# The scores of dense head group A as two split fp32r products over 128 partitions instead of one fp32 product over 64

## The chip, the cores and the metric

The kernel runs on one core of a Trainium2 chip. Its engines are named as in the profile: PE is TensorE (matrix products), with PEld its weight loads, DVE is VectorE, ACT is ScalarE, POOL is GpSimd, SP is SyncE, which issues the DMAs. The metric is the device time of one execution in microseconds; lower is better. Three runs of the kernel before took 1313.1, 1313.77 and 1316.71 us, median 1313.77.

## The reference

Two layers over 512 tokens of width 1024, all float32. Layer 0 mixes with attention, layer 1 with a recurrent block; each is followed by a SwiGLU feed-forward block, and a final RMS norm ends it. Only the attention's group A matters here: 8 query heads and 2 key heads of 64, each normalised per head, rotated by position, dense softmax over all 512 keys.

```python
a_q = _axial_rope(_rmsnorm(a_q, q_norm), row, col)
a_k = _axial_rope(_rmsnorm(a_k, k_norm), row, col)
...
s = jnp.einsum('bqgrd,bkgd->bgrqk', q_blk, k).astype(jnp.float32)
p = jax.nn.softmax(s, axis=-1).astype(v.dtype)
return jnp.einsum('bgrqk,bkgd->bqgrd', p, v)
```

Group B computes three dilated sliding-window attentions of 8 heads each from the same input projection and merges them by their softmax denominators.

## The kernel before

Every large product with weights is a split product, `mm3`: both operands are cut into a high part rounded to fp32r and a low part, the rest, and PE adds three fp32r products (high x high, high x low, low x high). A weight chunk comes by DMA into one of four stage buffers; ACT copies it to `w_hi` (L548), POOL subtracts to get `w_lo` (L488), PE waits for `chunk_lo` and uses it, and `chunk_used` lets ACT overwrite the slot. ACT and POOL convert chunk c + 4 while PE is at chunk c.

The order of work is written out by hand, one program per engine, in steps that are the weight chunks. The input projection is done in four head pairs p = 0 to 3 of 24 chunks (steps j = 0 to 23), and the attention is laid between the chunks. `A_SCORES = {10: 0, 13: 1, 16: 2, 19: 3}` puts the four score steps of group A (block c of 128 queries, two heads each) at steps 10, 13, 16 and 19 of pair p, `A_TURN` the transposes of their probabilities three steps later. `B_SCORES` puts the band scores of pair p - 1 at steps 0, 2, 4 and 6. Four more pieces of group B and of the output projection follow as p = 4. So there are 16 score steps of group A. A score step is, on PE, two fp32 products (one for each head of the pair: 64 partitions of `aq_f`, 128 queries, times 64 partitions of `ak`, 512 keys) into two banks; on DVE the maximum over both banks (`a_step`); on ACT two exponentials (`a_exps`); on DVE the normalisation (`a_normalise`); on PE the transposes (`a_turn`). The transposes of step c - 1 stand right ahead of the scores of step c on PE.

`aq_f` holds the rotated queries of pair p, two heads over 128 partitions. `ak` holds the two key heads, each copied by ACT (L675, two copies at step 9 and two at step 11 of pair 0) onto both halves of the partitions, so that either head of a pair finds its keys on its own partitions. DVE rotates the queries of the next pair at step 15 (`aq_rope`).

POOL and DVE also rotate group B's queries and keys of the pair: products with sine and cosine on POOL (L497, L503), a shuffle (L1098) and a sum on DVE (`rope_add`: `bq` L1109, `bkf` L1116, `bkn` L1111). The last `bkn` sum stands at step 22, and the band scores at step 0 of the next pair (L1600) wait for it (`roped`).

Of the kernel before, what the change touches and what calls it, by code (L numbers as in the profile page):

```python
# [5 lines left out]
P = 128  # L6
D = 1024
T = 512
KD = D // P
NC = T // P  # L10
# [199 lines left out]
def build(nc, A, out):  # L210
# [4 lines left out]
    with ctx:  # L215
# [4 lines left out]
        def at(name, off, shape, dt=f32):  # L220
            return nc.alloc_sbuf_tensor_at(name, [P] + list(shape), dt, offset=base + int(off))
# [45 lines left out]
        vf, bvf = at("vf", Z + 70.5 * K, [5 * P]), at("bvf", Z + 73 * K, [5, P])  # L267
        bvn = at("bvn", Z + 75.5 * K, [NC, 2, P])
        aq_f = at("aq_f", Z + 79.5 * K, [4, T])
        ak, av = at("ak", Z + 87.5 * K, [2, T]), at("av", Z + 91.5 * K, [NC, P])  # L270
        o_hi, o_lo = at("o_hi", Z + 93.5 * K, [KD, T], f32r), at("o_lo", Z + 109.5 * K, [KD, T], f32r)
        table = at("table", Z + 125.5 * K, [K_ALL - K_COSA])

# [26 lines left out]
        def sem(name):  # L300
            return ctx.enter_context(nc.semaphore(name))
# [13 lines left out]
        spilled, x_back = sem("spilled"), sem("x_back")  # L315
        half_ones_set, v_f_in, k_f_in, sq_done, aq_scaled, v_a_turned, av_in = (sem(n) for n in (
            "half_ones_set", "v_f_in", "k_f_in", "sq_done", "aq_scaled", "v_a_turned", "av_in"))
        ssq_ready, qk_ms, qk_sqrt, k_diag, k_rb, k_roped, ak_done, aq_roped = (sem(n) for n in (
            "ssq_ready", "qk_ms", "qk_sqrt", "k_diag", "k_rb", "k_roped", "ak_done", "aq_roped"))
        qk_in, sin_done, cos_done, roped, v_in = (sem(n) for n in ("qk_in", "sin_done", "cos_done", "roped", "v_in"))  # L320
        a_scored, a_bias, a_exp, a_prob = (sem(n) for n in ("a_scored", "a_bias", "a_exp", "a_prob"))
        b_scored, b_masked, b_bias, b_exp, b_prob = (sem(n) for n in ("b_scored", "b_masked", "b_bias", "b_exp", "b_prob"))
# [39 lines left out]
        def turned_near(hh, b):  # L362

            near = ptn[:, hh, :, :].rearrange("p g (c b i) -> p g c b i", c=NC, b=4)
            return near[:, :, :, b, :], ps[:, 2 + hh, 256:512].rearrange("p (g c i) -> p g c i", g=2, c=NC)

        block = ctx.enter_context(nc.Block())


# [166 lines left out]
        def _(act):  # L536
# [112 lines left out]
            def first_pair(j):  # L649

                if j == 0:
                    act.wait_ge(chunk_used, C_PAIR)
                    act.wait_ge(params_ready, 1)
                    act.activation(v_f[:, :], ps[:, 5, :], ACT.Copy).then_inc(v_f_in, 1)
                    act.activation(k_f[:, :], ps[:, 4, :], ACT.Copy, scale=qk_gain[:, 1:2]).then_inc(k_f_in, 1)
                    act.activation(sq_qk[:, 4, :], ps[:, 4, :], ACT.Square).then_inc(sq_done, 1)
                if j in (1, 2):
                    for m in (2 * j - 2, 2 * j - 1):
                        act.wait_ge(aq_scaled, m + 1)
                        act.activation(sq_qk[:, m, :], ps[:, m, :], ACT.Square).then_inc(sq_done, 1)  # L660
                if j == 5:
                    act.wait_ge(v_a_turned, 1)
                    act.activation(av[:, :, :].rearrange("p c d -> p (c d)"), ps[:, 2, :], ACT.Copy).then_inc(av_in, 1)
                if j == 6:
                    act.wait_ge(qk_ms, 1)
                    act.activation(rstd_qk[:, :, :, :], rstd_qk[:, :, :, :], ACT.Sqrt).then_inc(qk_sqrt, 1)
                    act.activation(scratch[:, 7:8], ones[:, 0:1], ACT.Exp)
                if j == 7:
                    act.wait_ge(lam_exp_in, 1)
                    act.activation(sp[:, 1, :], sp[:, 1, :], ACT.Exp, scale=-1.0).then_inc(lam_exp, 1)  # L670
                if j in (9, 11):
                    m = (j - 9) // 2
                    act.wait_ge(k_roped, 1)
                    for half in (m, 1 - m):
                        act.activation(ak[half * HD:(half + 1) * HD, m, :], k_f[m * HD:(m + 1) * HD, :], ACT.Copy).then_inc(ak_done, 1)  # L675

            def evacuate_qk(p, i):

# [49 lines left out]
            def attention(p, j):  # L728
# [21 lines left out]
                    b_exps(p - 1, b)  # L750
                if (c := a_scores_at(p, j)) is not None:
                    a_exps(p, c)
                if p and j == A_OUT:
                    out_hi(2 * p - 2, p - 1)
                if p and j == (LAST_OUT if p == 4 else B_OUT):
# [129 lines left out]
        def _(dve):  # L885
# [138 lines left out]
            def first_pair(j):  # L1024
# [30 lines left out]
                if j == 8:  # L1055
                    dve.wait_ge(k_rb, 1)
                    V.tensor_tensor(k_f[:, :], k_f[:, :], ps[:, 3, :], ALU.mult).then_inc(k_roped, 1)

            def a_step(p, c):

                dve.wait_ge(a_scored, 4 * p + c + 1)
                step.done(V.reduce_max(a_stat[:, 0, :], ps[:, 0:2, :], AX.X))
                V.tensor_tensor(a_stat[:, 1, :], a_stat[:, 0, :], exp_scale_neg[:, p, c, :], ALU.mult).then_inc(a_bias, 1)  # L1063
# [70 lines left out]
            def attention(p, j):  # L1134
# [28 lines left out]
                    b_normalise(p - 1, bs)  # L1163
                if as_ is not None:
                    a_normalise(p, as_)
                if p and j == A_OUT:
                    out_lo(2 * p - 2, p - 1)
                if p and j == (LAST_OUT if p == 4 else B_OUT):
# [288 lines left out]
        def _(pe):  # L1457
# [86 lines left out]
                                         start=m == 0, stop=m == 1)  # L1544
                    last.then_inc(k_rb, 1)

            heads = [slice(0, HD), slice(HD, P)]

            def turn_banks_free(n):

                if n:
# [3 lines left out]
            def a_scores(p, c):  # L1555

                if c == 0:
                    pe.wait_ge(aq_roped, p + 1)
                    pe.wait_ge(ak_done, 2 if p < 2 else 4)
                    if p:  # L1560
                        pe.wait_ge(b_masked, 8 * p)
                else:
                    pe.wait_ge(a_exp, 8 * p + 2 * c)
                for hh, r in enumerate(heads):
                    last = pe.matmul(ps[:, hh, :], aq_f[r, p, c * P:(c + 1) * P], ak[r, p // 2, :], start=True, stop=True)  # L1565
                last.then_inc(a_scored, 1)

            def a_turn(p, c):
# [335 lines left out]
```

## Time and profile before

| | |
|---|---|
| median of three runs | 1313.77 us |
| profiled execution, device time | 1317.05 us |
| its span in the trace | 1315.3 us |
| mean granted PE clock | 0.997 |
| PE busy | 1294.1 us, 6561 instructions |
| DVE busy | 544.1 us, 878 instructions |
| ACT busy | 541.1 us, 990 instructions |
| POOL busy | 603.7 us, 487 instructions |
| score products L1565 | 64 records (four to a step), 81.2 to 339 us |

The attention lies between about 50 and 390 us of the span; what follows is the feed-forward blocks and the recurrent layer. The trace gives, for every instruction, its start and its length, and for idle time the instruction that ended it. PE's records overlap, since its products are pipelined: what one costs is read from the distance between starts, not from its length. Line numbers are those of the kernel before unless said otherwise.

### The profile page before, as it was taken

The numbers are of one execution on the slowest core, as the hardware profiler recorded it, in microseconds if no ns is written. First come the engines' busy times: TensorE is split into PE (matmuls) and PEld (weight loads), VectorE is DVE, ScalarE is ACT, GpSimd is POOL, SyncE is SP. The second block draws the span as 40 slices with busy tenths as digits, with TensorE's granted clock in tenths as the row PEclk, the third lists the DMA queues.
The fourth block names the chain that finished last, engine by engine and source line by source line (L and its number), as shares of the span: only waits on it lengthen the run. The fifth ranks groups of instructions, "written<-read, shape, count | busy, mean of one in ns | idle before, by whom it ended". The sixth has DMA issues, their size and how long they took to land.

```text
span 1315.3 us, 18422 instructions
## 1 busy us (share of the span) xinstructions
PE 1294.1 (98%) x6561; PEld 1036.3 (79%) x6561; DVE 544.1 (41%) x878; ACT 541.1 (41%) x990; POOL 603.7 (46%) x487
## 2 busy tenths in 40 slices
PE   8999999999999999999999999999999999999998
PEld 6877786777778888888888877677788888888886
DVE  4456575665635331313111036999742121211021
ACT  4354444444435333333333245786433333333233
POOL 3465473555625444444444543530244545454442
PEclk9999999999999999999999999999999999999999
DMA  5522222121323333333333344214233333333232
GB/s 174 184 67 66 62 61 67 54 68 55 103 80 107 90 89 103 95 98 95 103 97 96 96 152 136 73 57 151 88 89 98 99 98 96 96 112 96 97 96 96
DMA packets 123351, 126.31 MB, mean 96 GB/s; under 512 B 7832, under 2 KB 106392, under 8 KB 122648
## 3 DMA queue, kind: packets, MB, share of 16 engines
q1 hardware_dynamic: 123256, 125.46, 31.6%
q8 instruction: 40, 0.66, 0.2%
q14 instruction: 23, 0.19, 0.0%
q10 hardware_dynamic: 32, 0.01, 0.0%
HBM read 119.15 MB, written 6.29 MB: 95 GB/s over the span
## 4 chain that ended last, share of the span: by engine, by line
PE 59%; issue 21%; POOL 12%; DVE 6%; ACT 2%; POOLq 0%; DMA 0%; SPq 0%; DVEq 0%; ACTq 0%
PE ps L1460 17%; PE ps L1462 16%; PE ps L1461 16%; POOL w_lo L488 11%; PE ps L1841 2%; PE ps L1588 1%; PE ps L1623 1%; PE ps L1600 1%; PE ps L1565 1%; PE ps L1604 1%; POOL rot L497 1%; PE ps L1634 1%; PE ps L1642 1%; DVE bkn L1111 1%; DVE gelu_g L1368 0%
## 5 line engine op out<-in xcount | busy, mean ns | idle before, releaser
L488 POOL TENSOR_TENSOR w_lo<-w_stage,w_hi 128x512 fp32r<-128x512 f32 (+2 forms) x430 | 537.5, 1254 | 695.9 <-ACT w_hi L548 695.5
L548 ACT ACTIVATE w_hi<-w_stage 128x512 fp32r<-128x512 f32 (+2 forms) x448 | 264.6, 594 | 622.4 <-PE ps L1462 615.8
L1460 PE MATMUL ps<-h_hi,w_hi 128*128 128x512 f32 x1104 | 441.1, 400 | 3.3 <-DVE h_lo L929 1.2
L1461 PE MATMUL ps<-h_lo,w_hi 128*128 128x512 f32 x1104 | 430.9, 390 | 0.0
L1462 PE MATMUL ps<-h_hi,w_lo 128*128 128x512 f32 x1104 | 430.8, 390 | 0.0
L1460 PEld LDWEIGHTS ps<-h_hi,w_hi 128*128 128x128 f32 x1104 | 207.7, 188 | 64.4 <-issue 14.3
L1462 PEld LDWEIGHTS ps<-h_hi,w_lo 128*128 128x128 f32 x1104 | 207.6, 188 | 44.2
L1461 PEld LDWEIGHTS ps<-h_lo,w_hi 128*128 128x128 f32 x1104 | 207.8, 188 | 42.6 <-issue 2.4
L1248 DVE TENSOR_TENSOR silu_g<-ps,rstd_wide 128x512 f32<-128x512 f32 x44 | 30.1, 685 | 327.4 <-PE ps L1462 327.4
L1460 PE MATMUL ps<-w_hi,f_hi 128*128 128x512 f32 x176 | 68.6, 390 | 0.1
L1461 PE MATMUL ps<-w_lo,f_hi 128*128 128x512 f32 x176 | 68.5, 389 | 0.0
L1460 PE MATMUL ps<-f_hi,w_hi 128*128 (+1 forms) x176 | 68.5, 389 | 0.0
L1462 PE MATMUL ps<-f_hi,w_lo 128*128 (+1 forms) x176 | 68.5, 389 | 0.0
L1462 PE MATMUL ps<-w_hi,f_lo 128*128 128x512 f32 x176 | 68.5, 389 | 0.0
L1461 PE MATMUL ps<-f_lo,w_hi 128*128 (+1 forms) x176 | 68.5, 389 | 0.0
L1183 DVE TENSOR_TENSOR x_t<-x_t,ps 128x512 f32<-128x512 f32 x24 | 15.8, 681 | 119.6 <-PE ps L1462 119.6
L1208 DVE TENSOR_TENSOR y_tok<-y_tok,ps 128x512 f32<-128x512 f32 x8 | 5.2, 684 | 98.7 <-PE ps L1462 98.7
L712 ACT ACTIVATE prob_a<-ps,a_stat,exp_scale 128x512 f32<-128x512 f32 x32 | 24.6, 774 | 46.0 <-DVE a_stat L1063 46.0
L1460 PEld LDWEIGHTS ps<-w_hi,f_hi 128*128 128x128 f32 x176 | 33.0, 188 | 7.3 <-POOL w_lo L488 0.5
L1461 PEld LDWEIGHTS ps<-f_lo,w_hi 128*128 128x128 f32 x176 | 33.0, 188 | 6.9
L1462 PEld LDWEIGHTS ps<-w_hi,f_lo 128*128 128x128 f32 x176 | 33.0, 188 | 6.9
L1460 PEld LDWEIGHTS ps<-f_hi,w_hi 128*128 128x128 f32 x176 | 33.0, 188 | 6.9
(223 smaller groups left out, 1621.8 us busy)
## 6 DMA issues: line engine op xcount, KB each, us to landing
w_stage<-in_ffn_w_gate_up_dram SPq DMA_DIRECT2D x176, 256.0 KB, 3.1
w_stage<-in_ffn_w_down_dram SPq DMA_DIRECT2D x88, 256.0 KB, 2.7
w_stage<-in_even_w_in_dram SPq DMA_DIRECT2D x96, 192.0 KB, 2.5
w_stage<-in_odd_w_in_dram SPq DMA_DIRECT2D x32, 256.0 KB, 2.7
x_spill<-x_t SPq DMA_DIRECT2D x2, 2048.0 KB, 7.9
x_t<-x_spill SPq DMA_DIRECT2D x2, 2048.0 KB, 8.0
w_stage<-in_odd_w_out_dram SPq DMA_DIRECT2D x16, 256.0 KB, 2.8
w_stage<-in_even_w_out_dram SPq DMA_DIRECT2D x16, 192.0 KB, 2.4
```

The lines of the kernel that those rows point to most:

```text
L488: pool.tensor_tensor(out=w_lo[:, s, 0:n], in0=stage[:, s, 0:n], in1=w_hi[:, s, 0:n].bitcast(f32), op=ALU.subtract).then_inc(chunk_lo, 1)
L497: pool.tensor_tensor(out=rot[:, g, :], in0=q_f[:, g, :], in1=tab(K_SINB, T), op=ALU.mult).then_inc(sin_done, 1)
L548: act.activation(w_hi[:, j % RING, 0:n], stage[:, j % RING, 0:n], ACT.Copy).then_inc(chunk_hi, 1)
L712: act.activation(prob_a[:, hh, :], ps[:, hh, :], ACT.Exp, scale=exp_scale[:, p, c, hh:hh + 1], bias=a_stat[:, 1, hh:hh + 1], accum_out=a_s ...
L1111: V.tensor_tensor(bkn[:, g - 1, :], q_f[:, g, :], rot[:, g, :], ALU.add).then_inc(roped, 1)
L1183: V.tensor_tensor(x_t[:, j, :], x_t[:, j, :], ps[:, b0 + m, :], ALU.add).then_inc(x_new, 1)
L1248: V.tensor_tensor(silu_g[:, q, :], ps[:, b0 + q, :], rstd_wide[:, :], ALU.mult).then_inc(gate_scaled, 1)
L1460: pe.matmul(out_, lh, rh, start=start, stop=False, skip_group_check=skip)
L1461: pe.matmul(out_, lh, rl, start=False, stop=False, skip_group_check=skip)
L1462: return pe.matmul(out_, ll, rh, start=False, stop=stop, skip_group_check=skip)
L1565: last = pe.matmul(ps[:, hh, :], aq_f[r, p, c * P:(c + 1) * P], ak[r, p // 2, :], start=True, stop=True)
L1841: last = pe.matmul(ps[:, 4 + q, :], gates[:, x, 2 * m + q // 2, q % 2, :], u_f[:, 2 * m + q // 2, :], start=True, stop=True)
```

## The change

The rotated queries of a pair are cut into high and low parts by ACT (`q_high`) and DVE (`q_low`), and stacked: `q_st0` has head 0's high part on its own 64 partitions and its low part on the other 64, `q_st1` likewise for head 1. `k_hi` has a key head's high part on both halves (ACT, in the place of `ak`), `k_lo` its low part on both halves (DVE, `k_low`, new). A head's scores are then two fp32r products over 128 partitions that add into one bank: stacked queries times `k_hi`, and stacked queries times `k_lo`. PE waits for `q_lo_done` and `k_lo_done` where it waited for `aq_roped` and `ak_done`.

```diff
+        q_st = [at("q_st0", Z + 99.5 * K, [T], f32r), at("q_st1", Z + 115.5 * K, [T], f32r)]
+        k_hi = at("k_hi", Z + 87.5 * K, [2, T], f32r)
+        k_lo = [at("k_lo0", Z + 107.5 * K, [T], f32r), at("k_lo1", Z + 123.5 * K, [T], f32r)]
...
                     for half in (m, 1 - m):
-                        act.activation(ak[half * HD:(half + 1) * HD, m, :], k_f[m * HD:(m + 1) * HD, :], ACT.Copy).then_inc(ak_done, 1)
+                        act.activation(k_hi[half * HD:(half + 1) * HD, m, :], k_f[m * HD:(m + 1) * HD, :], ACT.Copy).then_inc(k_hi_done, 1)
+
+            def q_high(p):
+
+                act.wait_ge(aq_roped, p + 1)
+                if p:
+                    act.wait_ge(a_scored, 4 * p)
+                for hh, r in enumerate(heads):
+                    act.activation(q_st[hh][r, :], aq_f[r, p, :], ACT.Copy).then_inc(q_hi_done, 1)
...
+                if (p, j) == (0, 7):
+                    q_high(0)
+                if p < 3 and j == 20:
+                    q_high(p + 1)
...
+            def k_low(m):
+
+                dve.wait_ge(k_hi_done, 2 * m + 2)
+                for r in heads:
+                    V.tensor_tensor(k_lo[m][r, :], k_f[heads[m], :], k_hi[heads[m], m, :].bitcast(f32), ALU.subtract).then_inc(k_lo_done, 1)
+
+            def q_low(p):
+
+                dve.wait_ge(q_hi_done, 2 * p + 2)
+                for hh, r in enumerate(heads):
+                    V.tensor_tensor(q_st[hh][heads[1 - hh], :], aq_f[r, p, :], q_st[hh][r, :].bitcast(f32), ALU.subtract).then_inc(q_lo_done, 1)
...
+                if p == 0 and j in (9, 11):
+                    k_low((j - 9) // 2)
+                if (p, j) == (0, 8):
+                    q_low(0)
+                if p < 3 and j == 21:
+                    q_low(p + 1)
...
                 if c == 0:
-                    pe.wait_ge(aq_roped, p + 1)
-                    pe.wait_ge(ak_done, 2 if p < 2 else 4)
+                    pe.wait_ge(q_lo_done, 2 * p + 2)
+                    pe.wait_ge(k_lo_done, 2 if p < 2 else 4)
...
-                for hh, r in enumerate(heads):
-                    last = pe.matmul(ps[:, hh, :], aq_f[r, p, c * P:(c + 1) * P], ak[r, p // 2, :], start=True, stop=True)
+                for hh in range(2):
+                    queries = q_st[hh][:, c * P:(c + 1) * P]
+                    pe.matmul(ps[:, hh, :], queries, k_hi[:, p // 2, :], start=True, stop=False)
+                    last = pe.matmul(ps[:, hh, :], queries, k_lo[p // 2][:, :], start=False, stop=True)
```

Where the new instructions stand, in three places. First DVE in pair 0, steps 9 to 11, from a shuffle of group B's rope (`rot`) over the maximum of the first scores (`a_stat`) to the normalisation and the next shuffle. Before:

```order
L1098 STREAM_SHUFFLE rot<-rot 128x512 [waits sin_done]
L1062 TENSOR_REDUCE a_stat<-ps 128x2 [waits a_scored,dve_step]
L1063 TENSOR_TENSOR a_stat<-a_stat,exp_scale_neg 128x2 [waits dve_step]
L1098 STREAM_SHUFFLE rot<-rot 128x512 [waits sin_done]
L1068 RECIPROCAL a_stat<-a_stat 128x2 [waits a_exp]
L1070 TENSOR_SCALAR prob_a<-prob_a,a_stat 128x512 [waits dve_step]
L1070 TENSOR_SCALAR prob_a<-prob_a,a_stat 128x512
L1098 STREAM_SHUFFLE rot<-rot 128x512 [waits sin_done]
L1109 TENSOR_TENSOR bq<-q_f,rot 128x4x4x32 [waits dve_step,cos_done]
```

The same stretch of the changed kernel, in its own line numbers:

```order
L1129 STREAM_SHUFFLE rot<-rot 128x512 [waits sin_done]
L1082 TENSOR_TENSOR k_lo_104<-k_f,k_hi 64x512 [waits k_hi_done]
L1082 TENSOR_TENSOR k_lo_104<-k_f,k_hi 64x512
L1093 TENSOR_REDUCE a_stat<-ps 128x2 [waits a_scored,dve_step]
L1094 TENSOR_TENSOR a_stat<-a_stat,exp_scale_neg 128x2 [waits dve_step]
L1129 STREAM_SHUFFLE rot<-rot 128x512 [waits sin_done]
L1099 RECIPROCAL a_stat<-a_stat 128x2 [waits a_exp]
L1101 TENSOR_SCALAR prob_a<-prob_a,a_stat 128x512 [waits dve_step]
L1101 TENSOR_SCALAR prob_a<-prob_a,a_stat 128x512
L1129 STREAM_SHUFFLE rot<-rot 128x512 [waits sin_done]
L1082 TENSOR_TENSOR k_lo_105<-k_f,k_hi 64x512 [waits k_hi_done]
L1082 TENSOR_TENSOR k_lo_105<-k_f,k_hi 64x512
```

Two subtractions stand ahead of the maximum of the first scores, which PE cannot make before they are done, and two behind the third shuffle, ahead of the first `bq` sum.

Second DVE at the end of pair 0 (steps 20 to 22), from the normalised probabilities of the fourth score step over the rope sums `bkf` and `bkn` and the copy of transposed probabilities (`pta`). Before:

```order
L1070 TENSOR_SCALAR prob_a<-prob_a,a_stat 128x512
L1116 TENSOR_TENSOR bkf<-q_f,rot 128x4x4x16 [waits dve_step,cos_done,pads_zeroed]
L1116 TENSOR_TENSOR bkf<-q_f,rot 128x4x4x16
L1111 TENSOR_TENSOR bkn<-q_f,rot 128x512 [waits dve_step,cos_done]
L1121 COPY pta<-ps 128x4x128 [waits turned1]
L1111 TENSOR_TENSOR bkn<-q_f,rot 128x512 [waits dve_step,cos_done]
```

Now:

```order
L1101 TENSOR_SCALAR prob_a<-prob_a,a_stat 128x512
L1147 TENSOR_TENSOR bkf<-q_f,rot 128x4x4x16 [waits dve_step,cos_done,pads_zeroed]
L1147 TENSOR_TENSOR bkf<-q_f,rot 128x4x4x16
L1142 TENSOR_TENSOR bkn<-q_f,rot 128x512 [waits dve_step,cos_done]
L1088 TENSOR_TENSOR q_st_101<-aq_f,q_st_101 64x512 [waits q_hi_done]
L1088 TENSOR_TENSOR q_st_102<-aq_f,q_st_102 64x512
L1152 COPY pta<-ps 128x4x128 [waits turned1]
L1142 TENSOR_TENSOR bkn<-q_f,rot 128x512 [waits dve_step,cos_done]
```

The next pair's two query subtractions stand between the two `bkn` sums; it is so in pairs 0, 1 and 2.

Third PE at the first score step of pair 0, between two chunk products. Before:

```order
L1462 MATMUL ps<-h_hi,w_lo 128x512
L1565 MATMUL ps<-ak,aq_f 128x512 [waits ak_done,aq_roped]
L1565 MATMUL ps<-ak,aq_f 128x512
L1460 MATMUL ps<-h_hi,w_hi 128x512 [waits chunk_lo]
L1461 MATMUL ps<-h_lo,w_hi 128x512
```

Now:

```order
L1499 MATMUL ps<-h_hi,w_lo 128x512
L1601 MATMUL ps<-k_hi,q_st_101 128x512 [waits k_lo_done,q_lo_done]
L1602 MATMUL ps<-k_lo_104,q_st_101 128x512
L1601 MATMUL ps<-k_hi,q_st_102 128x512
L1602 MATMUL ps<-k_lo_104,q_st_102 128x512
L1497 MATMUL ps<-h_hi,w_hi 128x512 [waits chunk_lo]
L1498 MATMUL ps<-h_lo,w_hi 128x512
```

Two products became four, and the wait is for the subtractions on DVE.

## Rows read from the trace of the kernel before

**Rows 1.** The page's first part: busy us, share of span, instructions by engine.
```profile
PE 1294.1 (98%) x6561; PEld 1036.3 (79%) x6561; DVE 544.1 (41%) x878; ACT 541.1 (41%) x990; POOL 603.7 (46%) x487
```
**Rows 2.** Waits of PE, 40 to 390 us: who for whom, total us, times, longest.
```profile
PE ps L1577 <- DVE prob_a L1070: 1.7, 4, 0.4
...
PE ps L1600 <- DVE bkn L1111: 0.5, 3, 0.2
```
**Rows 3.** Timeline of DVE, end of pair 0: start, length, instruction, idle time before.
```profile
117.31 1.77 DVE L1111 TENSOR_TENSOR bkn<-q_f,rot 128x512 f32<-128x512 f32 x1
...
119.60 0.90 DVE L1111 TENSOR_TENSOR bkn<-q_f,rot 128x512 f32<-128x512 f32 x1
```
**Rows 4.** Groups by line, DVE: count, busy us, mean ns, idle before.
```profile
L1333 DVE TENSOR_TENSOR w_lo<-w_stage,w_hi 128x512 fp32r<-128x512 f32 x18 | 12.0, 679 | 1.8 <-ACT w_hi L548 1.7
```
**Rows 5.** Timeline of POOL, end of pair 0.
```profile
117.06 1.47 POOL L503 TENSOR_TENSOR q_f<-q_f,table 128x512 f32<-128x512 f32 x1
118.49 3.84 POOL L488 TENSOR_TENSOR w_lo<-w_stage,w_hi 128x384 fp32r<-128x384 f32 x3
```
**Rows 6.** Timeline of PE, a score step of pair 3 with its neighbours.
```profile
320.59 0.39 PE L1462 MATMUL ps<-h_hi,w_lo 128*128 128x512 f32 x1
320.82 1.04 PE L1577 MATMUL ps<-ident,prob_a 128*128 128x128 f32 x8
321.79 1.13 PE L1565 MATMUL ps<-ak,aq_f 64*128 64x512 f32 x4
322.85 0.50 PE L1460 MATMUL ps<-h_hi,w_hi 128*128 128x512 f32 x1
323.18 0.39 PE L1461 MATMUL ps<-h_lo,w_hi 128*128 128x512 f32 x1
```
**Rows 7.** Timeline of PE, transposes with chunk products right behind, pair 1.
```profile
192.38 1.03 PE L1577 MATMUL ps<-ident,prob_a 128*128 128x128 f32 x8
193.17 0.47 PE L1460 MATMUL ps<-h_hi,w_hi 128*128 128x512 f32 x1
193.49 0.39 PE L1461 MATMUL ps<-h_lo,w_hi 128*128 128x512 f32 x1
```
**Rows 8.** Timelines of ACT, POOL, PE and DVE around pair 0's first scores.
```profile
75.56 0.52 ACT L548 ACTIVATE w_hi<-w_stage 128x384 fp32r<-128x384 f32 x1 [1.39 <-PE ps L1462]
...
79.79 1.27 ACT L675 ACTIVATE ak<-k_f 64x512 f32<-64x512 f32 x2
...
80.94 1.27 POOL L497 TENSOR_TENSOR rot<-q_f,table 128x512 f32<-128x512 f32 x1
82.17 1.02 POOL L488 TENSOR_TENSOR w_lo<-w_stage,w_hi 128x384 fp32r<-128x384 f32 x1
...
81.24 1.13 PE L1565 MATMUL ps<-ak,aq_f 64*128 64x512 f32 x4
...
82.63 0.39 PE L1461 MATMUL ps<-h_lo,w_hi 128*128 128x512 f32 x1
...
82.48 1.23 DVE L1062 TENSOR_REDUCE a_stat<-ps 128x2 f32<-128x1024 f32 x1 [3.20 <-PE ps L1565]
```
**Rows 9.** Timelines of DVE and POOL, steps 11 and 12 of pair 0.
```profile
89.18 1.48 DVE L1109 TENSOR_TENSOR bq<-q_f,rot 128x512 f32<-128x512 f32 x1 [0.51 <-POOL q_f L503]
...
87.67 1.47 POOL L503 TENSOR_TENSOR q_f<-q_f,table 128x512 f32<-128x512 f32 x1
89.10 1.00 POOL L488 TENSOR_TENSOR w_lo<-w_stage,w_hi 128x384 fp32r<-128x384 f32 x1
```
**Rows 10.** Timeline of DVE, step 13 of pair 1.
```profile
168.48 1.22 DVE L1062 TENSOR_REDUCE a_stat<-ps 128x2 f32<-128x1024 f32 x1 [0.38 <-PE ps L1565]
```
**Rows 11.** Timeline of PE at the output projection, after its longest wait there.
```profile
387.93 0.50 PE L1460 MATMUL ps<-o_hi,w_hi 128*128 128x512 f32 x1 [1.88 <-DVE o_lo L1132]
```
**Rows 12.** Windows: length, busy us (instructions) by engine, granted clock, DMA share, GB/s.
```profile
389.00:393.00 4.00, 4.00 (x12) 3.13 (x11) 1.28 (x2) 0.53 (x1) 1.00 (x1) 0.57 0.12 38
0.00:10.00 10.00, 7.04 (x24) 5.65 (x24) 1.68 (x4) 4.94 (x8) 2.15 (x9) 1.00 0.80 268
```

More of the change, by code:

```diff
@@ L269, in build @@
         aq_f = at("aq_f", Z + 79.5 * K, [4, T])
-        ak, av = at("ak", Z + 87.5 * K, [2, T]), at("av", Z + 91.5 * K, [NC, P])
+        av = at("av", Z + 91.5 * K, [NC, P])
+        q_st = [at("q_st0", Z + 99.5 * K, [T], f32r), at("q_st1", Z + 115.5 * K, [T], f32r)]
+        k_hi = at("k_hi", Z + 87.5 * K, [2, T], f32r)
+        k_lo = [at("k_lo0", Z + 107.5 * K, [T], f32r), at("k_lo1", Z + 123.5 * K, [T], f32r)]
         o_hi, o_lo = at("o_hi", Z + 93.5 * K, [KD, T], f32r), at("o_lo", Z + 109.5 * K, [KD, T], f32r)
@@ L317, in build @@
             "half_ones_set", "v_f_in", "k_f_in", "sq_done", "aq_scaled", "v_a_turned", "av_in"))
-        ssq_ready, qk_ms, qk_sqrt, k_diag, k_rb, k_roped, ak_done, aq_roped = (sem(n) for n in (
-            "ssq_ready", "qk_ms", "qk_sqrt", "k_diag", "k_rb", "k_roped", "ak_done", "aq_roped"))
+        k_hi_done, k_lo_done, q_hi_done, q_lo_done = (sem(n) for n in ("k_hi_done", "k_lo_done", "q_hi_done", "q_lo_done"))
+        ssq_ready, qk_ms, qk_sqrt, k_diag, k_rb, k_roped, aq_roped = (sem(n) for n in (
+            "ssq_ready", "qk_ms", "qk_sqrt", "k_diag", "k_rb", "k_roped", "aq_roped"))
         qk_in, sin_done, cos_done, roped, v_in = (sem(n) for n in ("qk_in", "sin_done", "cos_done", "roped", "v_in"))
@@ L365, in turned_near @@
             return near[:, :, :, b, :], ps[:, 2 + hh, 256:512].rearrange("p (g c i) -> p g c i", g=2, c=NC)
+        heads = [slice(0, HD), slice(HD, P)]
         block = ctx.enter_context(nc.Block())
@@ L1545, in first_pair @@
                     last.then_inc(k_rb, 1)
-            heads = [slice(0, HD), slice(HD, P)]
             def turn_banks_free(n):
```

## The prediction

> **What bounds the kernel now.** I read the views from the whole to the one place that the change touches. The engine table comes first: TensorE (PE) is busy in 98% of a span of 1315.3 us, VectorE (DVE) in 41%, ScalarE (ACT) in 41%, GpSimd (POOL) in 46% [rows 1]. Read alone, that says that a microsecond taken off PE is a microsecond off the time and that the other engines have room for anything. So I asked next for the waits of PE, for the attention alone (40 to 390 us): PE waits there for DVE's normalised probabilities (four times) and, at the first band scores of three of the four head pairs, for DVE's last rope sum `bkn` (three times) [rows 2]. The waits are short, 0.2 and 0.4 us, but they say that in the last third of a pair DVE ends level with PE. The timelines of DVE and POOL there show why: in pair 0 the sum `bkn` at 117.31 lasts 1.77 us, the next 0.90 [rows 3], while the same kind of instruction, two 512-wide inputs in SBUF, lasts 0.68 us when POOL is idle [rows 4]. POOL's product at 117.06 ends at 118.53, and 118.53 plus about 0.6 is the end of `bkn`; POOL's three `w_lo` then take 3.84 us instead of three times about 0.97 [rows 5]. The two engines take turns, a whole instruction at a time. So DVE's 41% is an average; from step 13 to step 23 of a pair its queue has no room, and what is put in it there moves the band scores.
>
> **What the change removes and adds on PE.** There are 16 score steps. One step now: transposes start at 320.82, scores at 321.79, the next chunk at 322.85, its second product at 323.18; normal products start 0.23 us apart [rows 6]. From the transposes to that second product: 2.36 us. Of this 1.06 is the two fp32 scores, and both passages (fp32 to fp32 with other rows, fp32 to fp32r) cost extra. After, four fp32r products stand in their place. A passage from transposes straight to fp32r is seen at 192.38, 193.17, 193.49 [rows 7]: 0.79 and 0.32 us. So the same stretch becomes 0.79 + 0.32 + 4 x 0.23 = 2.03 us, 0.33 less. The first step of pair 0 has no transposes ahead and gains 1.39 - 5 x 0.23 = 0.24 us. All sixteen: 15 x 0.33 + 0.24 = 5.2 us at most.
>
> The row speaks against a larger gain. The two scores of a step use 64 rows of the array each and end 1.06 us after they begin, 4.6 slots of 0.23 us, which is too little for two full fp32 products one after the other: they run side by side. The Trainium skill (FP8 and Floating Point Precision, on FP32 paths) says that true FP32 takes four passes through the array; counted for two products in a row that is eight slots, 1.82 us, and the change would save about 0.9 us a step, 14.6 us in all. The skill's TensorE page (TensorE: Matmul & The Clock Gate, Part 3 on packing small matmuls) says that matmuls on different row groups run at the same time, and that one of small K takes as long as one of K=128: filling 128 rows gives that up. By both together, four slots before and four after, nothing is saved but the passages; the row agrees with this.
>
> **What it adds on ACT.** Eight copies of 64 rows for the queries, 0.63 us each. The pair for pair 0 stands ahead of the conversion at 75.56, before which ACT is idle 1.39 us [rows 8]: 1.27 fits. Those of pairs 1 to 3 stand at step 20, before a conversion whose result POOL takes up 2 us later: no cost. The key copies stay.
>
> **What it adds on DVE: twelve subtractions of 64 rows, both inputs in SBUF.** Alone each holds DVE about 0.6 us (0.68 by its record [rows 4]). The trace shows no 64-row subtraction, so the lower bound is 0.6 each, the upper is 0.6 and a wait for one POOL instruction, 0.97 to 1.3. I take the upper wherever POOL has work ready, as the 1.77 us row does.
>
> - *First scores of pair 0.* The key copies on ACT run 79.79 to 81.06, and PE takes up the scores at 81.24 without a wait; DVE is idle 3.20 us until the scores' maximum at 82.48 [rows 8]. Now DVE must subtract twice in between. POOL's product runs 80.94 to 82.17; then DVE to 82.77, POOL's `w_lo` to 83.74, DVE to 84.34, scores at 84.4: PE stands 3.15 us. Without contention they are at 82.3, 1.1 us. Less the 0.24 of the cheaper scores: +2.9. The two query subtractions before it fall in DVE's idle time.
> - *Keys of the second group, step 11 of pair 0.* They stand between the shuffle and the first `bq` sum, in a chain that DVE ends late from here on. It has 0.51 us of idle time at that place, waiting for POOL's product of 87.67 [rows 9]. By turns (wait for that product, 0.6, `w_lo` 0.97, 0.6, wait 1.3 for the next product) the `bq` sum ends 2.5 us late; without contention 1.2 - 0.5 = 0.7. I take 2.5.
> - *Queries of the next pair, step 21 of pairs 0, 1 and 2.* They stand after the first `bkn` sum, ahead of a copy and the last `bkn` sum, behind which PE waits. POOL has three `w_lo` ready from 118.49 [rows 5]. By turns from 119.08: wait 0.97, 0.6, wait 0.97, 0.6, then the copy, then 0.1 more wait than now: the last `bkn` sum ends at about 123.75 instead of 120.5, +3.25 each, 9.75 in all. Without contention 1.2 each, 3.6. The row shows POOL ahead of DVE at this very place, so I take 3.25.
>
> **What of PE's gain is left.** In the stretches that DVE's chain ends, a faster PE only waits longer. In pair 0 none counts but the 0.24. In pairs 1 and 2 the chain last waits for PE at the scores of step 13 (0.38 us [rows 10]), so the 0.33 of the first step and 0.15 of the second (its scores end that much earlier) reach it: 2 x 0.48. In pair 3, without query work, I take 1.2 of 1.3. The sum: 2.9 + 2.5 + 9.75 - 0.96 - 1.2 = +13.0 us.
>
> **The clock.** PE now stands 3.3 us (pair 0) and, arriving earlier by its own gain, some 4.1 us (pairs 1 and 2) at the band scores. In the trace of before PE stands 1.88 us until 387.93, and from 389 to 393 its granted clock is 0.57 on average [rows 11, 12]: it fell from 2.4 to 1.2 GHz in most of that stretch, which lost 4 x 0.43 = 1.7 us. The first 10 us of the kernel, where PE is busy 7.04 of 10, show 1.00 [rows 12], so not every such time is followed by a fall. I count two falls of 1.6 us, after the two longest waits: +3.2. None counts 0, all three 4.8, one more for the wait at the first scores 6.4; what falls inside pair 0's DVE-bound stretch is hidden.
>
> Sum: +16.2 us on the profiled execution (1317.05 us, span 1315.3 and 1.75 around it) gives 1333.2. That execution was 3.3 us above the median of the three runs, 1313.77, so against the median: 1330.0 us.
>
> **Rivals.**
> 1. *DVE's chain with turns and falls of the clock* (forecast): 1330, own range 1325 to 1336. For it: the lengths 1.77 and 3.84.
> 2. *The same, and the clock stays up*: 1313.8 + 13.0 = 1326.8. For it the first 10 us; against it 389 to 393.
> 3. *64-row subtractions don't take turns with POOL.* Then 1.1 - 0.24 + 0.7 + 3 x 1.2 - 0.96 - 1.2 = +3.0, and with a fall or two of the clock up to +6: 1317 to 1320. Against it: every contended row is of the same kind with 128 rows, and nothing in them points to the rows.
> 4. *PE's gain decides* (the other side): DVE's additions vanish in its idle time, and the 5.2 us come out in full, 1308.6. It decides if each addition delays PE's next wait by less than 0.33 us a step. For it DVE's 41% and ACT's 41%; against it the waits for `bkn`, which leave 0.2 us where 1.2 is the least that is added.
> 5. *The scores do shrink by 0.9 us each*, by the eight slots above, and DVE's delays stand: 0.6 a step more than now wherever PE decides. In the four steps of pair 3 and the first two of pairs 1 and 2 that is 8 x 0.6, some 5 us: 1325. The 1.06 us rules it out nearly.
> 6. *That it doesn't do what it says*: two fp32r products of 128 rows take other than 0.23 us. The chunk products are of the same shape and type, so I give it next to nothing.
>
> **Chances.** Rival 1 0.50, rival 2 0.22, rival 3 0.14, rival 4 0.08, rivals 5 and 6 0.06 together. A measurement of this kernel tells 0.3%, 3.9 us, from no change. Faster: rival 4, 0.07. Within: half of rival 3 and a little of 4, 0.10. Slower: 0.83. The range leaves out rival 4 and the part of rival 3 below 1318, and reaches to three falls of the clock and 2 us of turns beyond the upper bounds: 1318 to 1337.
>
> **What would show it.** In the profile after: PE's score products at one start each 0.23 us and about 2.03 us from transposes to the second chunk product; a wait of PE of about 3 us for `k_lo` before the first scores; the waits for `bkn` grown from 0.2 to 3 or 4 us each, three of them; the pairs of subtractions at step 21 taking 1.6 us each by record; a granted clock below 1 in the microseconds after those waits; pair 3 about 1 us shorter than before; everything from the output projection on as before. Wrong it is if the pair of subtractions takes 1.3 us together beside POOL's work, if PE's wait at the band scores stays under 1.5 us, or if pairs 1 and 2 are no longer than they were.

## Result and the profile after

The changed kernel takes 1330.93 us (median of six runs, 1326.99 to 1331.83) beside 1314.34 us of the kernel before on the same chips: the ratio is 1.0116, 95% interval 1.0098 to 1.0134. It is slower by 16.6 us where 16.2 were forecast. The profiled execution took 1331.01 us, its span is 1329.2.

The first part of the page after, and the waits of PE from 40 to 410 us (who waited for whom, total us, times, longest):

```profile
PE 1293.6 (97%) x6561; PEld 1043.8 (79%) x6561; DVE 559.9 (42%) x890; ACT 545.7 (41%) x998; POOL 606.3 (46%) x487
```
```profile
PE ps L1637 <- DVE bkn L1142: 9.3, 4, 3.4
PE ps L1614 <- DVE prob_a L1101: 3.6, 6, 1.7
PE ps L1601 <- DVE k_lo L1082: 3.0, 1, 3.0
```

The averages say next to nothing: DVE went from 41% to 42% [rows 1]. The waits say all of it: the 0.5 us for `bkn` [rows 2] became 9.3 us, the 1.7 us for `prob_a` 3.6 us, and 3.0 us for `k_lo` are new. To see where the time is, I cut the trace of before and after at the same instructions: PE's arrival at the first scores, and the first band scores behind each pair. The columns are the stretch, its length, PE busy (instructions), granted clock, DMA share, GB/s. Before:

```profile
81.24:120.56 39.32, 38.31 (x223) 1.00 0.23 66
120.56:197.84 77.28, 76.30 (x561) 1.00 0.22 62
197.84:275.09 77.25, 76.25 (x562) 1.00 0.22 62
275.09:351.34 76.25, 75.87 (x561) 1.00 0.22 63
```

After:

```profile
79.60:127.59 47.99, 40.50 (x224) 0.93 0.22 62
127.59:208.58 80.99, 76.54 (x562) 0.98 0.21 59
208.58:289.95 81.37, 76.63 (x562) 0.98 0.21 59
289.95:366.90 76.95, 76.31 (x561) 0.98 0.20 58
```

Pair 0 is 8.67 us longer, pair 1 3.71, pair 2 4.12, pair 3 0.70: 17.2 us. The head and the tail of this execution are each 1.6 us shorter. The head is scatter between executions: in the profiled runs below, which leave it almost as it is, PE arrives at the first scores anywhere from 79.1 to 81.6 us. The tail is a matter of the clock. Before, the clock falls twice in it, at 389 us and here (window, columns as above):

```profile
788.00:793.00 5.00, 5.00 (x19) 0.66 0.96 349
```

After, it falls once, at 404 us. In all the traces of this document the tail lasts 960.6 to 960.8 us where it has no fall, 962.1 to 962.3 with one and 963.8 to 964.0 with two (the last 5 us of a trace, where all of them show a low clock, left aside). So a fall costs 1.6 us there, and the number of falls differs from one execution to the next.

Clock and waits belong together in the pairs too: the three stretches at 0.98 are those that begin behind a wait for `bkn`, and the 0.93 of pair 0 is two falls, behind the 2.99 us for `k_lo` and behind 1.73 us for `prob_a` at 109.60.

The score step on PE, from transposes to the second chunk product of pair 3, for [rows 6] (timeline: start, length, instruction):

```profile
353.17 1.04 PE L1614 MATMUL ps<-ident,prob_a 128*128 128x128 f32 x8
353.97 0.47 PE L1601 MATMUL ps<-k_hi,q_st 128*128 128x512 f32 x1
354.28 0.39 PE L1602 MATMUL ps<-k_lo,q_st 128*128 128x512 f32 x1
...
354.97 0.39 PE L1497 MATMUL ps<-h_hi,w_hi 128*128 128x512 f32 x1
355.20 0.40 PE L1498 MATMUL ps<-h_lo,w_hi 128*128 128x512 f32 x1
```

2.03 us, as worked out, against 2.36. PE's gain is real. DVE at the ends of pairs 0 and 1, for [rows 3], and PE behind the first:

```profile
120.97 1.78 DVE L1142 TENSOR_TENSOR bkn<-q_f,rot 128x512 f32<-128x512 f32 x1
122.78 2.81 DVE L1088 TENSOR_TENSOR q_st<-aq_f,q_st 64x512 fp32r<-64x512 f32 x2
...
126.22 1.31 DVE L1142 TENSOR_TENSOR bkn<-q_f,rot 128x512 f32<-128x512 f32 x1
...
202.51 1.78 DVE L1142 TENSOR_TENSOR bkn<-q_f,rot 128x512 f32<-128x512 f32 x1
...
207.75 0.77 DVE L1142 TENSOR_TENSOR bkn<-q_f,rot 128x512 f32<-128x512 f32 x1
```
```profile
127.59 1.17 PE L1637 MATMUL ps<-bkf,bq 64*128 64x256 f32 x4 [2.29 <-DVE bkn L1142]
```

From the end of the first `bkn` (122.75) to the end of the last (127.53) it is 4.78 us; before it was 1.42 (119.08 to 120.50). So the two subtractions cost 3.36 us in pair 0, of which 1.2 are their own work. In pair 1 it is 204.29 to 208.52, 4.23 us, so 2.8: the last sum takes 0.77 us there instead of 1.31. At the first scores (DVE, then PE), for [rows 8]:

```profile
79.41 3.06 DVE L1082 TENSOR_TENSOR k_lo<-k_f,k_hi 64x512 fp32r<-64x512 f32 x2 [0.64 <-ACT k_hi L682]
```
```profile
82.61 0.47 PE L1601 MATMUL ps<-k_hi,q_st 128*128 128x512 f32 x1 [2.99 <-DVE k_lo L1082]
...
83.44 0.63 PE L1602 MATMUL ps<-k_lo,q_st 128*128 128x512 f32 x1
83.87 0.63 PE L1497 MATMUL ps<-h_hi,w_hi 128*128 128x512 f32 x1
```

The starts go from 0.23 to 0.43 us apart at 83.4: PE's clock fell to 1.2 GHz here too, behind a wait of 2.99 us.

How much of this reaches DVE's chain is read from DVE's instructions behind it, for [rows 9]: the third shuffle before, then the same shuffle and the first `bq` sum after.

```profile
87.92 0.74 DVE L1098 STREAM_SHUFFLE rot<-rot 128x512 f32<-128x512 f32 x1
```
```profile
88.31 0.76 DVE L1129 STREAM_SHUFFLE rot<-rot 128x512 f32<-128x512 f32 x1
...
92.52 1.67 DVE L1140 TENSOR_TENSOR bq<-q_f,rot 128x512 f32<-128x512 f32 x1
```

Counted from PE's arrival at the first scores, the shuffle ends 2.05 us later than before (9.47 for 7.42) and the sum 5.17 us later (14.59 for 9.42). So the first scores put 2.05 us into the chain and the keys of the second group 3.1; the first `bkn` sum is still 5.3 us late, and the query subtractions add the last 3.36.

### The profile page after: what moved, and what is told of

Its sections match the earlier page's. It is cut to its first block, busy times and chain, and to the rows that moved or that the text cites. A ratio compares the mean times of both kernels' runs of the same rounds, so it can differ in the third digit from the quotient of the medians.

```text
span 1329.2 us, 18445 instructions
## 1 busy us (share of the span) xinstructions
PE 1293.6 (97%) x6561; PEld 1043.8 (79%) x6561; DVE 559.9 (42%) x890; ACT 545.7 (41%) x998; POOL 606.3 (46%) x487
## 4 chain that ended last, share of the span: by engine, by line
PE 58%; issue 20%; POOL 11%; DVE 8%; ACT 2%; POOLq 0%; DMA 0%; SPq 0%; ACTq 0%; DVEq 0%
PE ps L1497 16%; PE ps L1499 16%; PE ps L1498 16%; POOL w_lo L495 10%; PE ps L1878 2%; PE ps L1625 1%; PE ps L1637 1%; PE ps L1660 1%; PE ps L1641 1%; DVE bkf L1147 1%; DVE q_st L1088 1%; PE ps L1671 1%; DVE bkn L1142 1%; DVE a_stat L1093 1%; PE ps L1679 1%
## 5 line engine op out<-in xcount | busy, mean ns | idle before, releaser
L735 ACT ACTIVATE prob_b<-prob_b,b_stat 128x512 f32<-128x512 f32 x32 | 22.9, 716 | 41.1 <-DVE b_stat L1113 41.1
L1499 PEld LDWEIGHTS ps<-f_hi,w_lo 128*128 128x128 f32 x176 | 33.0, 188 | 6.9
```

The lines of the kernel that those rows point to most:

```text
L735: act.activation(prob, prob, ACT.Exp, scale=SCALE, bias=b_stat[:, b % 2, 1, hh:hh + 1], accum_out=b_stat[:, b % 2, 2, hh:hh + 1]).then_inc ...
L1499: return pe.matmul(out_, ll, rh, start=False, stop=stop, skip_group_check=skip)
```

## Experiments

The theory: the added subtractions lengthen DVE's chain by their own work and by the turns that DVE and POOL take; behind the waits that this makes the clock falls; PE's gain mostly goes into waits, since DVE sets the end of a pair. The rivals: the time is in the new products; or only in the length of the added work; or the clock doesn't matter.

| run | edit | median us | ratio to before (95%) |
|---|---|---|---|
| the changed kernel | | 1330.93 | 1.0098 to 1.0134 |
| q_late | query split in its own pair | 1318.45 | 1.0013 to 1.0033 |
| keys | key split moved | 1326.32 | 1.0071 to 1.0099 |
| psum | one SBUF input less | 1325.31 | 1.005 to 1.0086 |
| warm | products inside the waits | 1325.51 | 1.0064 to 1.009 |
| work_only | old products, new work | 1331.52 | 1.01 to 1.0131 |
| moved | q_late and keys | 1314.48 | 0.9981 to 1.0003 |
| tiled | moved, three products on 64 rows | 1314.15 | 0.9978 to 0.9996 |
| rope_before | before, rotation at step 5 | 1313.4 | 0.9983 to 1.0004 |
| rope_moved | moved, rotation at step 5 | 1316.43 | 1.0008 to 1.0035 |
| rope_tiled | tiled, rotation at step 5 | 1314.05 | 0.9988 to 1.0006 |
| rope7_moved | moved, rotation at step 7 | 1320.48 | 1.0036 to 1.006 |
| rope7_tiled | tiled, rotation at step 7 | 1315.51 | 0.9993 to 1.001 |

The kernel before had medians of 1314.14 to 1315.34 us beside them.

**q_late: the query split where DVE has time.**

```diff
-                if (p, j) == (0, 7):
-                    q_high(0)
-                if p < 3 and j == 20:
-                    q_high(p + 1)
+                if p < 4 and j == 7:
+                    q_high(p)
...
-                if (p, j) == (0, 8):
-                    q_low(0)
-                if p < 3 and j == 21:
-                    q_low(p + 1)
+                if p < 4 and j == 8:
+                    q_low(p)
```

> The query split of every pair at steps 7 (ACT) and 8 (DVE) of its own pair, where DVE has idle time, instead of steps 20 and 21 of the pair before. Theory (the subtractions lengthen DVE's chain by 3.25 us each in three pairs, and the clock falls behind the waits): the waits for bkn are back at 0.2 to 1.5 us, no clock fall behind them, 9.75 + about 4.8 us and about 1.5 us of PE's own gain come back: 1315 us (1313 to 1318). Rival (only the length of the instructions counts, 1.2 us a pair): 1326 to 1328. Rival (the time went elsewhere, into the four products of a score step): 1331, no change.

1318.45 us: 12.5 us come back for moving six subtractions and their copies, nothing left out. It is the largest single piece. It stands a little above the range's top. One reason is PE's gain, of which little came back: pairs 1 to 3 last 77.05, 77.05 and 75.66 us, with the clock at 1.00 in all three, against 77.28, 77.25 and 76.25 before. The other is pair 0, which gives back 2.5 us where 3.25 were summed: DVE's last `bkn` sum ends at 123.47, but PE, whose clock fell twice in this pair, comes only at 124.55. The rival of four slow products is out.

**keys: the key split moved.**

```diff
-                if j in (9, 11):
-                    m = (j - 9) // 2
+                if j in (8, 11):
+                    m = (j - 8) // 3
...
-                if p == 0 and j in (9, 11):
-                    k_low((j - 9) // 2)
                 if (p, j) == (0, 8):
+                    k_low(0)
+                if (p, j) == (1, 7):
+                    k_low(1)
+                if (p, j) == (0, 7):
                     q_low(0)
```

> Only the keys' split moved: ACT copies the first group's high parts at step 8 ahead of a conversion, DVE subtracts at step 8 and pair 0's queries at step 7; the second group's subtractions in step 7 of pair 1. Theory: PE's wait of 3.0 us at the first scores falls to under 0.5, its clock fall goes (1.7 us, perhaps hidden), and the chain in pair 0 is 2.5 us shorter: 1331 - 3.0 - 2.5 = 1325.5, down to 1324 with the clock. Rival (pair 0 is ended by something else, DVE's rope sums with POOL, whatever stands ahead): 1329 to 1331.

1326.32 us, 4.6 less. PE's wait at the first scores is 0.36 us, and pair 0 (from PE's arrival, 81.13) lasts 42.70 us at a clock of 1.00, 5.3 less than in the changed kernel and 3.4 more than before, which is the wait for `bkn` that was left in. Windows of pairs 0 to 2, columns as above:

```profile
81.13:123.83 42.70, 37.10 (x222) 1.00 0.24 70
123.83:203.32 79.49, 75.01 (x561) 1.00 0.21 61
203.32:284.70 81.38, 76.63 (x561) 0.98 0.21 59
```

Pair 1 begins behind a wait for `bkn` of 3.35 us and pair 2 behind one of 3.36; behind the first the clock held, behind the second it fell. So a wait of this length is not followed by a fall every time.

**psum: the same length of work, without turns.** The low parts of pairs 1 to 3 are not the queries' here, since the second input is a PSUM bank.

```diff
-                    V.tensor_tensor(q_st[hh][heads[1 - hh], :], aq_f[r, p, :], q_st[hh][r, :].bitcast(f32), ALU.subtract)
+                    V.tensor_tensor(q_st[hh][heads[1 - hh], :], aq_f[r, p, :], ps[r, 4, :] if p else q_st[hh][r, :].bitcast(f32), ALU.subtract)
```

> As the changed kernel, but the three query subtractions of pairs 1 to 3 take their second input from a PSUM bank that nobody writes then (so the low parts are wrong numbers): the same length of work on DVE, one SBUF input less. Theory (DVE and POOL take turns only where DVE reads two SBUF inputs): the two take 1.3 us together instead of 2.8, the waits for bkn shrink by about 2 us each, 1331 - 6 = 1325 us, 1323 if a clock fall goes too. Rival (the length and the place count, not the turns): 1331.

Timeline of DVE at the end of pair 0:

```profile
124.50 1.40 DVE L1088 TENSOR_TENSOR q_st<-aq_f,ps 64x512 fp32r<-64x512 f32 x2
```

1.40 us for the two (and in pair 1 again) instead of 2.81, the waits for `bkn` 5.6 us in all instead of 9.3, the time 1325.31, 5.6 less. So the turns with POOL are shown, and their price is about that of the work itself. The runs of this kernel spread from 1321.61 to 1330.14, and its profile, the slowest of them, has this in pairs 1 to 3:

```profile
127.41:206.01 78.60, 75.01 (x562) 1.00 0.22 62
206.01:287.87 81.86, 78.00 (x561) 0.96 0.21 59
287.87:366.13 78.26, 77.62 (x561) 0.96 0.20 59
```

Behind the wait of 0.42 us the clock held, behind the two of 2.46 us it fell, and for longer than in the changed kernel. So the clock's part varies from run to run, and the spread is most likely that.

**warm: PE kept busy inside its waits.**

```diff
                 if b == 0:
-                    pe.wait_ge(roped, 7 * (q + 1))
                     pe.wait_ge(a_exp, 8 * (q + 1))
+                    if q < 3:
+                        for _ in range(9):
+                            pe.matmul(ps[:, 0, :], h_hi[:, 0, 0:P], h_hi[:, 0, :], start=True, stop=True)
+                    pe.wait_ge(roped, 7 * (q + 1))
```

> As the changed kernel, with nine fp32r products of 512 columns (2.05 us, their result is overwritten) put on PE ahead of its wait for bkn in three pairs, inside that wait. Theory (the clock falls because PE stands still, each fall costs 1.6 us): the granted clock stays at 1.00 behind the three waits, 1331 - 4.8 = 1326 us, or 1328 if only two of the three go. Rival (behind the band scores DVE's steps decide and a slower PE is hidden): 1331.

1325.51 us, 5.4 less: PE does 27 products more and the kernel is faster. The clock is 1.00 in all three stretches:

```profile
127.03:206.56 79.53, 77.09 (x571) 1.00 0.21 61
206.56:286.38 79.82, 77.11 (x570) 1.00 0.21 60
286.38:361.70 75.32, 74.58 (x561) 1.00 0.20 59
```

They are 1.46, 1.55 and 1.63 us shorter than after the change, the price that one fall had in [rows 12], 1.7. The rival that a slower PE is hidden behind the band scores is out.

**work_only: the added work with the old products.**

```diff
-                    pe.matmul(ps[:, hh, :], queries, k_hi[:, p // 2, :], start=True, stop=False)
-                    last = pe.matmul(ps[:, hh, :], queries, k_lo[p // 2][:, :], start=False, stop=True)
+                    last = pe.matmul(ps[:, hh, :], aq_f[r, p, c * P:(c + 1) * P], k_hi[r, p // 2, :].bitcast(f32), start=True, stop=True)
```

> All the copies, subtractions and waits of the change, where it puts them, but the scores are again one fp32 product over 64 partitions a head, from aq_f and k_hi (with the keys' high part alone, so the result lacks the low part). It tells the added work from the new products. Theory: the time is that of the changed kernel and a little, since PE's gain reaches the end in few places: 1331 + 0.2 (pair 0) + 2 x 0.2 + 0.6 (what pairs 1 to 3 gained where the query split was moved away) = 1332 us, 1330 if a clock fall less comes of the shorter waits; the waits for bkn 2.3 to 3.4 us. Rival (the four products in place of two cost the time): near 1315.

1331.52 us. With the old products and the new work the time is the changed kernel's; the products that were the point of the change hardly move it, either way.

**moved: both moves.** The edits are those of q_late and keys, with pair 0's query subtraction at step 7.

> Both moves together: query splits at steps 7 and 8 of their own pair, keys' first group at step 8, second group in step 7 of pair 1. Theory: no wait for k_lo above 0.5 us, chain of pair 0 as before, waits for bkn 0.2 to 0.5 us: 1318.5 - 4.6 = 1313.9 us beside 1315.2 for the kernel before; of PE's 5.2 us only about 1 reaches the end, because DVE's chain of steps 13 to 23 ends level with PE. Rival (PE's gain comes out in full once the added work is hidden): 1310.

1314.48 us beside 1315.34, ratio 0.9992 (0.9981 to 1.0003): all 16.6 us are accounted for by the place of the work, and no gain is left that can be told from none. PE's waits:

```profile
PE ps L1612 <- DVE prob_a L1099: 3.4, 6, 1.5
PE ps L1495 <- ACT q_f L699: 2.3, 3, 0.8
PE ps L1635 <- DVE bkn L1140: 1.9, 4, 0.6
```

Before these three were 1.7, 1.1 and 0.5 us: 4.3 us of PE's 5.2 are waits now.

**tiled: three products a head on 64 rows.**

```diff
-                for hh in range(2):
-                    queries = q_st[hh][:, c * P:(c + 1) * P]
-                    pe.matmul(ps[:, hh, :], queries, k_hi[:, p // 2, :], start=True, stop=False)
-                    last = pe.matmul(ps[:, hh, :], queries, k_lo[p // 2][:, :], start=False, stop=True)
+                for i, (low, keys) in enumerate(((0, k_hi[:, p // 2, :]), (0, k_lo[p // 2][:, :]), (1, k_hi[:, p // 2, :]))):
+                    for hh, r in enumerate(heads):
+                        last = pe.matmul(ps[:, hh, :], q_st[low][r, c * P:(c + 1) * P], keys[r, :], start=i == 0, stop=i == 2)
```

> As moved, but the scores as three fp32r products a head over 64 partitions (high x high, high x low, low x high), the two heads on their own rows and issued in turn; the query split is then one 128-partition copy and one subtraction. If products on different rows run side by side, as the fp32 pair did, a score step is 3 slots of 0.23 instead of 4: 0.7 us, and half the DVE work of the query split goes. Since DVE's chain ends level with PE, the time moves less than 16 x 0.23 = 3.7: 1312 to 1314. Rival (fp32r products on different rows don't overlap): 6 slots, 1.4 us a step, 1316 to 1320.

```profile
320.23 1.03 PE L1609 MATMUL ps<-ident,prob_a 128*128 128x128 f32 x8
321.19 0.50 PE L1597 MATMUL ps<-k_hi,q_st 64*128 64x512 f32 x2
321.53 0.40 PE L1597 MATMUL ps<-k_lo,q_st 64*128 64x512 f32 x2
321.77 0.39 PE L1597 MATMUL ps<-k_hi,q_st 64*128 64x512 f32 x2
322.09 0.50 PE L1493 MATMUL ps<-h_hi,w_hi 128*128 128x512 f32 x1
322.42 0.39 PE L1494 MATMUL ps<-h_lo,w_hi 128*128 128x512 f32 x1
```

Two products on different rows take one slot, so the side by side holds for fp32r. But the passages cost more than to 128-row products: 0.96 and 0.34 us on the way in, 0.32 and 0.33 on the way out. The step is 2.19 us, worse than the 2.03 of the change and better than the 2.36 of before. The time is 1314.15 us, 0.9987 (0.9978 to 0.9996); it differs from before by less than the 0.3% that I called no change.

**rope_before, rope_moved, rope_tiled: take the rotation out of the chain.** If DVE's chain holds PE's gain back, DVE's 3.8 us of group A's rotation should go where DVE waits.

```diff
-                if p < 3 and j == 15:
-                    aq_rope(p + 1)
+                if 0 < p < 4 and j == 5:
+                    aq_rope(p)
```

> The kernel before with one edit: DVE rotates group A's queries of a pair at step 5 of that pair, where DVE waits for PE, instead of step 15 of the pair before, inside the chain that ends level with PE. Theory (DVE's chain of steps 13 to 23 sets pairs 0 to 2): a pair lasts 76.25 us, as pair 3 without that work does, instead of 77.27: 1315.3 - 3 = 1312.3. Rival (PE alone sets the pairs): no change, or slower by what the rotation delays at step 6.

> The changed kernel with all its splits moved (as moved), and the rotation at step 5 as well. Theory: pairs 0 to 2 last 75.7 us as pair 3 of moved does, instead of 77.07: 1314.5 - 4.1 = 1310.4 us, so that of the cheaper scores more reaches the end: 2 us between this and rope_before, the 5.2 us not in full since the last bkn sum still ends behind PE. Rival (the gain was lost elsewhere than in DVE's chain): 1314.

> As rope_moved, with the scores as three products a head on 64 rows each, side by side, and the query split as one copy and one subtraction. A score step with its transposes took 2.19 us there against 2.03, but DVE has 0.6 us less to do a pair: PE-bound now, it should be 16 x 0.16 = 2.6 us slower than rope_moved if PE sets the time, equal if DVE does: 1310 to 1313.

1313.4, 1316.43 and 1314.05 us, where 1312.3, 1310.4 and 1310 to 1313 were forecast. The first half of the theory held, the forecast of the time did not. Pair 0 shows the first half. From PE's arrival at the first scores it lasts 39.32 us before and 39.91 in moved, but 37.84 in rope_before and 36.99 in rope_moved:

```profile
81.48:118.47 36.99, 36.63 (x223) 1.00 0.25 71
```

Here the rotation no longer stands in the chain, and the cheaper scores reach the end of the pair, 0.85 us of them. Pairs 1 to 3, which now have a rotation at step 5, don't gain: 77.18, 77.21 and 77.19 us in rope_before. In rope_moved PE waits no more for `prob_a`, but

```profile
PE ps L1495 <- ACT q_f L699: 7.8, 3, 2.6
```

The rotation at step 5 stands ahead of DVE's fourth band mask. ACT waits for that mask, and behind its wait stands the evacuation of `q_f`, without which PE has no bank (timelines of ACT and PE, pair 2):

```profile
224.93 0.72 ACT L735 ACTIVATE prob_b<-prob_b,b_stat 128x512 f32<-128x512 f32 x1 [4.12 <-DVE b_stat L1111]
```
```profile
229.22 0.76 PE L1495 MATMUL ps<-h_hi,w_hi 128*128 128x512 f32 x1 [2.61 <-ACT q_f L699]
```

In rope_before, where ACT has no query copies at step 7, the same wait is 3.9 us in all. rope_moved also shows what a fall of the clock costs, in one execution: the clock fell behind the waits of 2.6 us in pairs 1 and 2 and held behind the same wait in pair 3, and the pairs last 79.06, 78.99 and 77.47 us.

**rope7_moved, rope7_tiled: the rotation at step 7, the query split at step 9.**

> As rope_moved, with the rotation two steps later (step 7, behind the last band score step of DVE) and the query split of pairs 1 to 3 at step 9 behind ACT's evacuation of the rope inputs. In rope_moved the rotation held DVE's fourth band mask back by 3 us, ACT waited 4.1 us for it and evacuated q_f late: PE waited 2.6 us a pair and its clock fell. Theory: that wait is back at 0.4 us, none for prob_a, bkn under 0.3: PE sets the pairs, 75.7 us each: 1310.5 us (1309 to 1312). Rival (whatever is moved, DVE and ACT end level with PE somewhere else): 1314.

> As rope7_moved with the scores as three products on 64 rows, two heads side by side (2.19 us from transposes to the second chunk product against 2.03). If PE sets the pairs now: 16 x 0.16 = 2.6 us slower than rope7_moved, 1313. If DVE still does, its smaller query split makes it equal or faster: 1310.

1320.48 and 1315.51 us, where 1310.5 and at most 1313 were forecast. `q_f` is back at 1.1 us, and in rope7_moved the next in line is the query split itself, now too near to the scores:

```profile
PE ps L1599 <- DVE q_st L1086: 6.0, 3, 2.1
```

My error was to count the rotation at 3 us and the split at 1.3; in this place both take turns with POOL (timeline of DVE, pair 2):

```profile
231.01 1.66 DVE L1038 TENSOR_TENSOR aq_f<-aq_f,rot_a 128x512 f32<-128x512 f32 x1
...
234.04 2.70 DVE L1086 TENSOR_TENSOR q_st<-aq_f,q_st 64x512 fp32r<-64x512 f32 x2
```

In pair 1 something else comes on top. The rotation stands behind the key split of step 7 there, and behind both stands DVE's copy that frees a bank for PE's transposes of the band probabilities (L1156, done at 154.98). Timeline of PE, rope7_moved:

```profile
155.09 1.06 PE L1658 MATMUL ps<-ident,prob_b 128*128 128x128 f32 x8 [2.94 <-issue]
```

The profile names no releaser for this wait. That it is the copy is read from the program's order and from the copy's end, 0.1 us ahead; no run tests it. rope7_tiled has the same wait, 2.95 us, and a fall of the clock behind it. Its pairs 1 and 2:

```profile
117.97:198.22 80.25, 76.92 (x571) 0.98 0.21 60
198.22:274.62 76.40, 75.30 (x570) 1.00 0.22 63
```

So 3.9 us of rope7_tiled are this collision in one pair; without it the estimate is 1311.7, inside the forecast, and no run has it apart. For rope7_moved the rival was right: the work, moved once more, made PE wait in a new place. For rope7_tiled these runs don't decide.

## Why the prediction was right, step by step

*PE's gain, 0.33 us a step.* Right: 2.03 us from transposes to the second chunk product, as summed. The row won over a count of passes: the two fp32 products had run side by side.

*ACT at no cost.* Right: in the trace after, no wait of PE or DVE is put down to the query copies.

*First scores, 3.15 us.* Measured 2.99, and gone to 0.36 when the keys were moved. As a wait of PE it was right; as a term of the sum, 2.9, it was too large, since DVE's chain was only 2.05 us late behind it. Its next instructions took less time than before: the two normalisations 0.88 us instead of 1.65.

*Keys of the second group 2.5, queries 3.25 each.* Pair 0 as a whole was to be 2.9 + 2.5 + 3.25 = 8.65 us longer, measured 8.67. That this is so near is luck: the three parts are 2.05, 3.1 and 3.36, and the rest is 0.1. In pair 1 the query subtractions cost 2.8, a little under the term. That they cost more than their own 1.2 us because of the turns is shown by psum. The Trainium skill states the rule (SBUF — State Buffer, section Who interferes with whom): a DVE instruction with two SBUF inputs contends with a GpSimd instruction that reads SBUF, and the loser waits for the whole instruction. The trace agrees: 2.81 us a pair with two SBUF inputs, 1.40 with one. The waits that PE was to have at the band scores, 3.3 us in pair 0 and some 4.1 in the others, were 2.29 and 3.35: the chain was less late in pair 1 than summed, and in pair 0 PE came later itself, after two falls of its clock (in keys, without them, its wait there is 3.35).

*PE's gain that is left, 0.48 in pairs 1 and 2 and 1.2 in pair 3.* This was a mis-sized term. q_late and moved show the pairs without the added waits, but with the query split inside them: 0.2, 0.2 and 0.6 us shorter than before. warm, whose pair 3 has no query work, as in the changed kernel, and no fall of the clock, shows 0.9 for it (75.32 for 76.25). In pair 3 I had taken PE for the one that sets the end; it waited for `bkn` 0.27 us there instead. That makes 0.9 us that the sum had too much of gain.

*The clock, two falls of 1.6 us.* Three fell, and warm shows 1.5, 1.6 and 1.6 us for them. It is the second mis-sized term, by 1.4. Pair 0 had two falls more, behind the first scores and behind 1.73 us for `prob_a`, and the second the prediction did not have at all. They were nearly hidden in DVE's chain, as said: the chain is 5.3 us late ahead of the second fall (the copy of `pta` at 112.49, before 108.82) and 5.3 us late behind it (`bkn` at 120.97, before 117.31).

*The sum.* With the measured terms, pair 0 is 8.67, pairs 1 and 2 are 2.8 - 0.2 each (for 3.25 - 0.48), pair 3 is -0.9 and the clock 4.6: 17.6 us, and the four pairs of the profiled execution are 17.2 us longer. The head and the tail of that execution took 3.3 us off again, which no run ties to the change; between the two profiled executions, on which the sum was made, the difference is 14.0 us (1331.01 for 1317.05). By medians it is +16.6 for +16.2. That nearness is in part luck: the gain and the falls of the clock were off in one direction, by 2.3 us, the subtractions of pairs 1 and 2 in the other, by 0.9, and how many falls an execution has in its tail is scatter.

*The rivals.* Rival 2 is out by the falls that warm takes away, rival 3 by 2.81 us beside 1.40, rival 4 by moved, in which no gain is left even with the added work out of the way, and rivals 5 and 6 by the step of 2.03 us.

## What to carry to other kernels

Before a product is made cheaper by preparing its operands, ask on which queue the preparation stands and what ends behind it: here 5.2 us were taken off the engine that is busy 98%, and the kernel became 16.6 us slower through one that is busy 41%, because the preparation stood ahead of instructions for which the first engine was about to wait. The same work, moved to steps in which its engine waits, cost nothing that could be measured; and a wait of a few microseconds on PE should be counted with what its clock loses behind it.

## What the runs showed of the hardware

- Two-input SBUF subtractions of 64 partitions take turns with POOL just as those of 128 do, and last as long: 0.69 us for one that POOL does not hold up (keys, before the first scores), 2.8 to 3.1 us for two beside POOL. With one input in PSUM they don't, 1.40 us for two.
- Two fp32r products on different 64 rows of the array take one slot of 0.24 us, and so share it as two fp32 products do. A passage from 128-row transposes to 64-row products costs about 0.2 us more than to 128-row products.
- In the changed kernel PE's clock fell to 1.2 GHz behind waits of 1.73, 1.88, 2.29, 2.99 and twice 3.35 us. The three falls at the band scores cost 1.5 to 1.6 us each; with nine products in the waits they did not come.
- The length of the wait does not decide it. In keys the clock held behind 3.35 us and fell behind 3.36, in rope_moved it fell behind two waits of 2.6 us and held behind a third; behind the wait of 1.88 us for `o_lo` it fell before and in moved, and held in q_late and warm. In psum two falls behind waits of 2.46 us lasted twice as long as the others. I can't tell from these runs which waits are followed by a fall and for how long.
